# Gate and up projections of 32 experts as three products of rounded parts, with tokens stationary

## The reference, cut to what matters

```python
hg = einsum('nd,edf->nef', x, w_gate[g])      # D = 1024 -> 256
hu = einsum('nd,edf->nef', x, w_up[g])        # D = 1024 -> 256
a = silu(hg) * hu * gate[:, g, :, None]
y = y + einsum('nef,efd->nd', a, w_down[g])   # 256 -> D
```

## Time and profile before

| what | us |
|---|---|
| median of three runs | 1079.71 |
| the profiled execution, its own time | 1078.85 |
| its span, first to last instruction | 1076.4 |
| stage of the experts (first gate and up to last down) | 628.8 to 1007.8 |
| tail (last down to end) | 68.6 |
| first use of GB2, from the span's start (L1229) | 1030.5 |
| loads of GB2, issue to landing | 7.2 and 10.7 |
| busy PE, DVE, ACT, POOL over the span | 959.2, 381.8, 271.5, 93.5 |
| mean granted clock of TensorE | 0.952 |

### The profile page before, as it was taken

One profiled execution on the slowest core, in us unless ns is written; L12 is line 12 of the kernel. 1 busy time (PEld: TensorE's weight loads), 2 busy tenths in 40 slices (PEclk: granted clock), 3 DMA queues, 4 the chain that ended last, 5 costly groups with the idle time before them and its releaser, 6 DMA issues.

```text
span 1076.4 us, 15977 instructions
## 1 busy us (share of the span) xinstructions
PE 959.2 (89%) x6348; PEld 737.2 (68%) x6348; DVE 381.8 (35%) x839; ACT 271.5 (25%) x580; POOL 93.5 (9%) x146
## 2 busy tenths in 40 slices
PE   6999999968989998699997379999999999999584
PEld 6999889834555454478885368778878877887331
DVE  5202020187757776835444800010001001000066
ACT  5202110034434444722222011111111111111053
POOL 0000000400000000000000012112211211221000
PEclk9999999989989999899998579999999999999797
DMA  9999996599667575086225939999889999991354
GB/s 332 334 356 331 375 327 268 210 283 317 245 239 261 164 258 187 1 338 234 79 64 174 339 100 325 305 320 317 303 289 317 329 304 326 321 323 64 133 217 152
DMA packets 116279, 273.40 MB, mean 254 GB/s; under 512 B 13984, under 2 KB 82080, under 8 KB 113408
## 3 DMA queue, kind: packets, MB, share of 16 engines
q1 hardware_dynamic: 107456, 247.97, 66.5%
q0 software_dynamic: 8768, 24.66, 6.4%
HBM read 256.33 MB, written 95.30 MB: 327 GB/s over the span
## 4 chain that ended last, share of the span: by engine, by line
PE 79%; DVE 12%; issue 3%; DMA 3%; ACT 3%; SPq 0%; DVEq 0%; POOL 0%; POOLq 0%; ACTq 0%
PE psum L640 74%; PE psum L699 3%; DMA back<-pair_d 1%; DVE back L1219 1%; DVE back L1201 1%; DVE front L1465 1%; DVE back L488 1%; ACT front L1085 1%; DVE stats L1204 1%; PE psum L838 1%; DMA middle<-pair_d 0%; DVE middle L1229 0%; DVE middle L1551 0%; DVE wo_low L1335 0%; ACT back L987 0%
## 5 line engine op out<-in xcount | busy, mean ns | idle before, releaser
L640 PE MATMUL psum<-back,front 128*64 128x128 f32 (+2 forms) x1280 | 152.1, 307 | 14.4 <-DVE back L488 10.6
L640 PEld LDWEIGHTS psum<-back,front 128*64 128x64 f32 (+2 forms) x1280 | 110.4, 167 | 49.5 <-issue 29.0
L640 PE MATMUL psum<-front 64*128 64x512 f32 (+5 forms) x448 | 120.5, 507 | 11.1 <-DVE stats L1201 6.8
L640 PE MATMUL psum<-back 128*128 128x112 f32 (+3 forms) x1152 | 123.1, 307 | 0.8 <-issue 0.8
L640 PEld LDWEIGHTS psum<-back 128*128 128x128 f32 (+1 forms) x1152 | 111.0, 170 | 13.6 <-issue 6.6
L640 PE MATMUL psum<-back,middle 128*128 128x112 f32 (+1 forms) x880 | 101.8, 316 | 0.9 <-issue 0.9
L640 PE MATMUL psum<-x_high,w_high 128*128 128x352 f32 x288 | 94.1, 327 | 8.1 <-DVE w_low L356 8.1
L640 PEld LDWEIGHTS psum<-back,middle 128*128 128x128 f32 (+1 forms) x880 | 91.2, 181 | 13.8 <-issue 13.8
L640 PEld LDWEIGHTS psum<-front 64*128 64x128 f32 (+2 forms) x448 | 51.6, 191 | 65.0 <-issue 45.8
L640 PE MATMUL psum<-x_low,w_high 128*128 128x352 f32 x288 | 93.4, 324 | 0.0
L640 PE MATMUL psum<-x_high,w_low 128*128 128x352 f32 x288 | 93.2, 324 | 0.0
(11 more groups left out here) (185 smaller groups left out, 1173.9 us busy)
## 6 DMA issues: line engine op xcount, KB each, us to landing
out_win_k_s<-cache_win_k SPq DMA_DIRECT2D x16, 2044.0 KB, 13.7
out_win_v_s<-cache_win_v SPq DMA_DIRECT2D x16, 2044.0 KB, 12.1
front<-w_down SPq DMA_DIRECT2D x16, 1024.0 KB, 7.3
middle<-w_gate SPq DMA_DIRECT2D x16, 1024.0 KB, 5.6
back<-w_up SPq DMA_DIRECT2D x16, 1024.0 KB, 8.1
back<-winkT SPq DMA_DIRECT2D x8, 1792.0 KB, 7.8
back<-cache_win_v SPq DMA_DIRECT2D x8, 1024.0 KB, 7.4
front<-w_gate SPq DMA_DIRECT2D x8, 1024.0 KB, 5.7
```

Source lines behind the costliest of these rows:

```text
L640: return nc.tensor.matmul(out, lhsT, rhs, start=start, stop=stop, skip_group_check=True)
```

## The change

Gate and up are computed as in the projections. The tokens (112 columns of XGH or XGL) are stationary, the 512 columns of gate and up side by side are moving, and the result has tokens on partitions. For that

- SP loads gate and up as one array `w_gu`, in two halves of 8 KB per partition, three buffers deep; w_down in one piece of 8 KB per partition; GB2 only when gate and up of the last expert are done;
- ACT rounds the weights of expert e+2 (4 casts of 128x1024) and the tokens of e+1 (2 casts of 128x448, out of PSUM); DVE writes the low parts of both;
- the activation is transposed back on PE (2 transposes) and copied out of PSUM by DVE;
- down, and with it y and the scatter, run one expert behind;
- POOL reads the indices in place, without the copies of columns; its order stays.

The Fori loops are unrolled. The overflow branch is adapted in the same way as far as its buffers go. The diff, cut to its core:

```diff
 def gate_up(e):                                    # PE
+    pe.wait_ge(s_xl, 2 * e + 2)
+    if e >= 2:
+        pe.wait_ge(s_av, e - 1)
+    for k in range(KT):
+        if k % 2 == 0:
+            pe.wait_ge(s_wl, 4 * e + k // 2 + 1)
+        mm(o, xh[:, k, :], wh[:, k, :], k == 0, False)
+        mm(o, xh[:, k, :], wl[:, k, :], False, False)
+        last = mm(o, xl[:, k, :], wh[:, k, :], False, k == KT - 1)
+        if k % 4 == 3:
+            last.then_inc(s_gu, 1)
...
+gather_transposes(0)                               # waits s_gx
+for e in range(NE):
+    gate_up(e)
+    if e + 1 < NE:
+        gather_transposes(e + 1)
+    if e:
+        down(e - 1)                                # waits s_at, s_ya, s_yd
+    active_transposes(e)                           # waits s_av, s_at
+down(NE - 1)
...
+for e in range(NE):                                # ACT
+    silu(e)
+    if e + 1 < NE:
+        tokens_rounded(e + 1)                      # waits s_tp
+    if e + 2 < NE:
+        weights_rounded(e + 2)                     # waits s_gf, s_gu
+    if e:
+        y_half(e - 1)                              # waits s_y
...
+for e in range(NE):                                # DVE
+    if e:
+        active_out(e - 1)                          # waits s_tt
+    if e >= 2:
+        y_half(e - 2)
+    if e + 1 < NE:
+        weights_rest(e + 1)
+    active(e)
+    if e + 1 < NE:
+        tokens_rest(e + 1)
...
+gather(0)                                          # POOL
+gather(1)
+for e in range(NE):
+    if e + 2 < NE:
+        await_(s_tp, 2 * e + 2)
+        gather(e + 2)
+    pool.wait_ge(s_ya, e + 1)
+    await_(s_yd, e + 1)
+    scatter(e)
...
+for e in range(3, NE):                             # SP
+    for half in range(2):
+        sp.wait_ge(s_gu, 2 * (e - 3) + half + 1)
+        load_gu(sp, e, half)
+    if e >= 4:
+        sp.wait_ge(s_y, e - 3)
+        load_dn(sp, e)
```

More of the change, by code:

```diff
@@ L133, in build @@
         CATH, CATL = overlay("cat_high", 8448, KT, TOK), overlay("cat_low", 18576, KT, TOK)
+        GU_AT, GUH_AT = (0, 18576, 27024), (4096, 22672)
+        GUH = [overlay(f"gu_high{s}", GUH_AT[s], KT, 2 * DE) for s in range(2)]
+        GUL = [overlay(f"gu_low{s}", GU_AT[s], KT, 2 * DE) for s in range(3)]
+        XGH = [overlay(f"xg_high{s}", (33168, 16896)[s], KT, CAP) for s in range(2)]
+        XGL = [overlay(f"xg_low{s}", (34064, 13312)[s], KT, CAP) for s in range(2)]
         arenas = [(lo, hi, ctx.enter_context(nc.sbuf_tensor(name, [P, hi - lo], F32))) for name, lo, hi in
@@ L195, in build @@
         LG = at(13600, CH, 36)
[L197 to L204, removed]
+        GUF = [at(x, KT, 2 * DE) for x in GU_AT]
+        WD = [at(x, 2, D) for x in (11264, 44688, 46736, 48784)]
+        XG = [at(31120 + D * s, D) for s in range(2)]
+        SIL = [at(8192 + 256 * s, DE) for s in range(2)]
+        ACTV = [at(8704 + 256 * s, DE) for s in range(2)]
+        AT = [at(15872 + 256 * s, 2, P) for s in range(2)]
         YS = [at(9216 + D * s, D) for s in range(2)]
-        GB2 = at(11264, 2, D)
+        OXGT, OSIL = at(20624, KT, P), at(8192, 2, P)
+        GB2 = at(0, 2, D)
         YP = [at(off, 2, D) for off in (24720, 27024, 29072)]
@@ L456, in ring_load, with load_gu, load_dn @@
             return [at(off, DB * 2, D_C)], [I["cache_mem_v"].rearrange("b (t p) n -> p (b t) n", p=P)]
[L458 to L469, removed]
+        def load_gu(sp, e, half):
+            k = slice(4 * half, 4 * half + 4)
+            sp.dma_start(GUF[e % 3][:, k, :], I["w_gu"][e][:, k, :]).then_inc(s_gf[e % 3][half], 16)
+        def load_dn(sp, e):
+            sp.dma_start(WD[e % 4], I["w_down"][e]).then_inc(s_wd[e % 4], 16)
         R0 = 13600 + 324
@@ L478, in build @@
         RV = at(9216, 2, CH, 96)
-        OH = [at(32912 + P * s, P) for s in range(4)]
+        OH = [at(50832 + P * s, P) for s in range(4)]
         IDX = at(34960, 3 * NE).bitcast(U32)
@@ L584, in _ @@
             sp.wait_ge(s_mix, CH)
-            load_expert(sp, 0, 0)
+            for half in range(2):
+                load_gu(sp, 0, half)
+            load_dn(sp, 0)
             for c in range(CH - 3, CH):
                 store_h1(c)
[L588 to L598, removed]
+            for e in (1, 2):
+                for half in range(2):
+                    load_gu(sp, e, half)
+                load_dn(sp, e)
+            load_dn(sp, 3)
+            for e in range(3, NE):
+                for half in range(2):
+                    sp.wait_ge(s_gu, 2 * (e - 3) + half + 1)
+                    load_gu(sp, e, half)
+                if e >= 4:
+                    sp.wait_ge(s_y, e - 3)
+                    load_dn(sp, e)
             with overflow(sp):
@@ L609, in _ @@
                 sp.nop()
+            sp.wait_ge(s_gu, 2 * NE)
             for v, n in (("ln2_g", 0), ("ln2_b", 1)):
@@ L874, in gather_transposes @@
                         k = 4 * hf + j
-                        last = nc.tensor.transpose(bank(hf)[:, j * P:j * P + CAP], XG[sl][0:CAP, k * P:k * P + P], ident[0:CAP, 0:CAP])
+                        last = nc.tensor.transpose(bank(hf)[:, j * P:j * P + CAP], XG[e % 2][0:CAP, k * P:k * P + P], ident[0:CAP, 0:CAP])
                     last.then_inc(s_tp, 1)
[L878 to L884, removed]
@@ new lines, in active_transposes, with down @@
+            def active_transposes(e):
+                pe.wait_ge(s_av, e + 1)
+                if e:
+                    pe.wait_ge(s_at, e)
+                for f in range(2):
+                    last = nc.tensor.transpose(bank(6)[:, f * P:f * P + CAP], ACTV[e % 2][0:CAP, f * P:f * P + P], ident[0:CAP, 0:CAP])
+                last.then_inc(s_tt, 1)
+            def down(e):
+                pe.wait_ge(s_at, e + 1)
+                pe.wait_ge(s_wd[e % 4], 16 * (e // 4 + 1))
+                if e:
+                    pe.wait_ge(s_ya, e)
+                    pe.wait_ge(s_yd, e)
@@ L895, in _ @@
[L895 to L920, removed]
+            gather_transposes(0)
[3 more added lines that the diff above has]
+                    gather_transposes(e + 1)
+                if e:
+                    down(e - 1)
+                active_transposes(e)
@@ L1068, in _, with weights_rounded @@
             nc.scalar.activation(W2, W2, ACT.Exp).then_inc(s_ra, 1)
-            def expert(i, j, first):
-                e = i * 4 + j
+            def weights_rounded(e):
+                if e >= 2:
+                    act.wait_ge(s_gu, 2 * (e - 1))
+                for q in range(4):
+                    if q % 2 == 0:
+                        act.wait_ge(s_gf[e % 3][q // 2], 16 * (e // 3 + 1))
+                    k = slice(2 * q, 2 * q + 2)
+                    nc.scalar.copy(GUH[e % 2][:, k, :], GUF[e % 3][:, k, :]).then_inc(s_wh, 1)
@@ L1073, in expert, with tokens_rounded @@
+            def tokens_rounded(e):
                 for hf in range(2):
                     act.wait_ge(s_tp, e * 2 + (hf + 1))
[L1075 to L1086, removed]
@@ L1088, in y_half @@
-            def y_half(i, j, first):
-                e = i * 4 + j
-                act.wait_ge(s_y, e + 1)
[L1091 to L1094, removed]
-            act.wait_ge(s_idx, 1)
[L1097 to L1109, removed]
+                    if e >= 2:
+                        act.wait_ge(s_gu, 2 * (e - 1))
+                    nc.scalar.copy(XGH[e % 2][:, 4 * hf:4 * hf + 4, :],
+                                   bank(hf).rearrange("p (j n) -> p j n", j=4)[:, :, 0:CAP]).then_inc(s_xh, 1)
@@ new lines, in silu, with y_half @@
+            def silu(e):
+                act.wait_ge(s_gu, 2 * e + 2)
+                if e >= 2:
+                    act.wait_ge(s_av, e - 1)
+                nc.scalar.activation(SIL[e % 2][0:CAP, :], bank(2 + e % 2)[0:CAP, 0:DE], ACT.Silu).then_inc(s_sil, 1)
+            def y_half(e):
+                act.wait_ge(s_y, e + 1)
+                if e >= 2:
+                    act.wait_ge(s_ys[e % 2], 16 * (e // 2))
+                nc.scalar.activation(YS[e % 2][0:CAP, 0:512], bank(4)[0:CAP, :], ACT.Copy,
+                                     scale=GS[0:CAP, e:e + 1]).then_inc(s_ya, 1)
@@ L1113, in _ @@
                         act.wait_ge(o_tp, b * 2 + (hf + 1))
[L1114 removed]
+                        nc.scalar.copy(OXGT[:, 4 * hf:4 * hf + 4, :], bank(hf).rearrange("p (j n) -> p j n", j=4)).then_inc(o_xgt, 1)
                     act.wait_ge(o_gu, b + 1)
[L1116 removed]
+                    nc.scalar.activation(OSIL.rearrange("p a n -> p (a n)"), bank(2)[:, 0:256], ACT.Silu).then_inc(o_sil, 1)
                     act.wait_ge(o_y, b + 1)
@@ L1457, in _, with weights_rest, tokens_rest @@
             dve.sem_inc(s_idx, 1)
-            def turn(i, j, first):
-                e = i * 4 + j
-                dve.wait_ge(s_sil, e + 1)
-                if not first:
+            def weights_rest(e):
+                for q in range(4):
+                    dve.wait_ge(s_wh, 4 * e + q + 1)
```

(47 more changed lines are left out.)

71 lines of the change are left out of this document (41 added, 30 removed).

## The result

The changed kernel takes 1328.55 us (median of four runs, 1324.49 to 1332.48) against 1080.34 beside it: a ratio of 1.234, 95% interval 1.229 to 1.239. It is slower, as forecast, but by 248 us where 82 were forecast, and outside the range (1098 to 1205).

The account below looks back on a forecast made before the run. TensorE was taken to bound the kernel before. Expert 2's transposes at 645.2, plus 29 turns of 14.7 us, gave 1071.5; the last experts brought 1090.9, the tail a span of 1159.3, and 2.45 more the forecast 1162 us (range 1098 to 1205).

Parts of the forecast that it names:

- The loop: Experts: transposes, down, y, scatter, gather and landing close in 13.2 us per turn, against 11.75 before; TensorE waits 3.1.
- The new TensorE work: Experts: gate and up as 24 products in 5.53 us instead of 7.11; 10.06 us of TensorE per turn.
- The clock: Experts: the waits bring a low clock (1.2 GHz) on transposes and down, adding 1.5 us: 14.7 per turn.
- Scatter at S+7.1, 0.97 long: POOL: the scatter starts 7.1 us after S, the start of an expert's transposes, and takes 0.97 us.
- The rival: DVE's subtractions and POOL's DMAs hold each other up: up to 2.4 us per turn, 1197 to 1232 us; chance 0.14.
- Landing 5.0 after that: Gather's DMA: rows land 5.0 us after its issue at S+8.1, so S+13.1; bounds 4.1 and 8.0.
- Small terms: Links in the turn: 1.07 us from y to scatter, no gap between scatter and gather, 0.14 from landing to transposes.
- 1.6 less than now: Experts: TensorE's 10.06 us of work per turn was said to be 1.6 us below the kernel before.
- The short loop: Experts: preparation done while waiting, landing 4.1, no low clock: 11.5 us per turn, 1067.5 us; chance below 1074: 0.09.
- the edit as it is meant: Experts: gather never late, TensorE (10.06) or DMA (10.25 us per turn) bounds: 1031 us; chance 0.03.

Follow-up runs that it names:

- POOL's order: Changed kernel with POOL issuing the scatter of expert e-1 after the gather of e+2: 1037.93 us, ratio 0.964 to the kernel before.
- the filler: Changed kernel with eight float32 matmuls of constants into an unused PSUM bank ahead of the transposes: 1288.99 us.
- y first: On top of POOL's order, ACT's half of y moved ahead of its four weight casts: 1024.05 us, ratio 0.953 to the kernel before.
- subtractions first: Changed kernel with DVE's four subtractions of a turn ahead of its copy out and y: 1317.55 us.
- PSUM operand: Changed kernel with a constant PSUM bank as second operand of DVE's weight subtractions, so low parts are not the reference's: 1249.42 us.

## Why the prediction was wrong

**The loop: right.** "So the loop closes in 13.2 us, more than the 11.75 now" named the cause. TensorE waits at the transposes, released by the gather alone; giving the loop two turns by POOL's order, though neither DMA became fast, took 1328 to 1038.

**The new TensorE work: right.** 24 products in 5.56 and 5.58 us against 5.53, down 3.44, and a turn of 10.04 us against 10.06 where nothing else bounds.

**The clock: right in kind, a little low.** The low stretches came in every turn examined. From the transposes to the end of y it was 7.8 us (829.29 to 837.08 in the timeline) against the forecast 6.0 + 1.5; with the filler it was 6.0. So the clock cost 1.8 us a turn where 1.5 were forecast.

**"Scatter at S+7.1, 0.97 long": wrong, the largest error.** It took 4.56 us: 3.6 more per turn. The duration came from a trace in which DVE was idle at that moment. The forecast saw this and put it among the rivals, with a price of "From 0 to one subtraction (1.22) for each of two DMAs, up to 2.4 per turn". In the changed kernel that bound was wrong: the scatter waited for the last of the four subtractions. The gather behind it was not held up at all (0.99), since DVE was through by then. In the kernel with y first the bound held: one subtraction for each DMA, 1.7 us for both. The rival named the right mechanism and would have given 1232 at most.

**"Landing 5.0 after that": wrong by 1.9 us.** "I take the median, since a weight load is under way as before" did not look at which loads. In the kernel before, the nearest 1 MB load was some 4 us old when a gather went out. Now SP issues two of them in the 4 us ahead of it. The late scatter is not to blame for this: with the scatter at 0.97 us, and the gather 2.5 and 3.7 us earlier in the turn, the landing took 9.1 us (subtractions first) and 7.6 us (PSUM operand). Since the forecast's own gather, at S+8.1, also goes out just behind the middle of gate and up (S+7.5), where SP issues the first half, 5.0 would probably have been too short even with the scatter as forecast.

**Small terms.** Between scatter and gather 0.30 against 0; from y to the scatter 0.82 against 1.07; from the landing to the transposes 0.04 against 0.14. The sum of a turn: 14.7 + 0.25 (clock) - 0.25 (preparation) + 3.6 (scatter) + 0.3 (gap) + 1.9 (landing) - 0.1 = 20.4. The "1.6 less than now" should read 1.7 (11.75 - 10.06), which is also what y first shows (11.75 - 10.04); the forecast time does not rest on it.

**The short loop** (1067.5) and **the edit as it is meant** (1031) did not occur. The latter's figure was nearly reached by the kernel with POOL's new order, and passed by the one with y first.

The profile of before could have priced neither term, but the range could have: DVE's whole run of four (4.9 us) as the upper bound of the hold-up, and the largest landing (8.0) in place of the median, give 14.7 + 4.9 + 3.0 = 22.6 us a turn, 1391 us. Both upper ends were at hand, and the range left them out.

## What to carry to other kernels

When a stage is moved one turn later, look at every in-order queue for what stands behind its end: here a prefetch stood behind a store, and the gain in TensorE's work turned into a loop over POOL, DMA and back. Put prefetches ahead of stores in the queue's order, and finish what frees a consumer (y) before work for two turns ahead (the casts). Where a duration is taken from a trace in which the neighbour was idle, take as the upper bound the neighbour's whole uninterrupted run. Where a landing is taken from another kernel, look at what is issued in the few us ahead of it.

## What was unexpected of the hardware

- POOL's indirect scatter takes 0.97 us alone and 4.56 us beside four back-to-back DVE subtractions with both operands in SBUF; with one operand in PSUM it is 0.97 again, DVE's durations being the same. In another order of ACT's work, beside four subtractions just as close together, it takes 1.66 us.
- An indirect gather of up to 112 rows of 4 KB lands in 4.6 us (4.0 to 5.1) with no load issued in the several us ahead, and in 9.1 us in the median when issued between two of 1 MB.
- Two single improvements can cancel: moving DVE's work out of the scatter's way brought the gather forward by 2.4 us a turn, and the later landing took all but 0.3 of it back.
- Filling TensorE's wait with useless matmuls raised the granted clock from 0.76 to 0.99 in the experts and saved 40 us.
